# Conversion by token groups between the stages, and feed-forward products with the weights standing

## The reference, cut to what matters

```python
# first block
x = layer_norm(ALPHA * x + attention_mixer(x))      # D -> q, k, v, g ; g gates ; D -> D
x = layer_norm(ALPHA * x + retention_mixer(x))      # 8 heads of q, k (256), v, g (512)
# second block (RMS norms, modulated by c @ w_mod: scale, shift, gate of each half)
h = rms_norm(x) * (1 + scale_a) + shift_a
x = x + gate_a * (mix(h @ w_in) @ w_out)            # window and selected-key attention
h = rms_norm(x) * (1 + scale_f) + shift_f
u, g = split(h @ w_up)                              # 2 x 5632 columns
u = causal_conv3(u) + conv_b
x = x + gate_f * ((silu(u) * g) @ w_down)
out = rms_norm(x)
```

## Time and profile before

| what | value |
|---|---|
| time, median of three runs (2285.35 to 2291.1) | 2290.98 us |
| time of the profiled execution | 2291.69 us |
| span of that execution, first to last instruction | 2290.0 us |
| PE busy | 97% |
| PE weight load busy | 80% |
| DVE busy | 74% |
| ACT busy | 43% |
| mean rate of the loads | 220 GB/s |

### The profile page before, as it was taken

The page is one execution under the profiler, slowest core; times in us unless marked ns, Lnnn a source line. Parts: engine busy times, 40 slices in busy tenths (PEclk is TensorE's granted clock), DMA queues, the critical chain, the costliest instruction groups (busy, mean ns, idle before and its releaser), DMA issues.

```text
span 2290.0 us, 28816 instructions
## 1 busy us (share of the span) xinstructions
PE 2230.9 (97%) x10634; PEld 1842.1 (80%) x10634; DVE 1702.5 (74%) x1908; ACT 995.1 (43%) x1017; POOL 141.6 (6%) x202
## 2 busy tenths in 40 slices
PE   7999999999999999999999999999999999999998
PEld 6878887787888888888787778778888888888886
DVE  6788887988868878688795666985665667665567
ACT  4443433534434334343343455454444444444444
POOL 2110010010000000000011001000000000000000
PEclk9999999999999999999999999999999999999999
DMA  7877775697777777787646546455555556555653
GB/s 266 284 258 257 255 263 209 211 330 267 273 263 269 271 262 279 248 277 267 245 152 211 177 139 172 141 167 183 186 190 193 183 183 195 189 183 183 192 190 132
DMA packets 260288, 503.57 MB, mean 220 GB/s; under 512 B 14705, under 2 KB 68385, under 8 KB 259328
## 3 DMA queue, kind: packets, MB, share of 16 engines
q1 hardware_dynamic: 228480, 381.73, 50.2%
q0 software_dynamic: 31376, 119.80, 15.0%
q10 hardware_dynamic: 368, 1.18, 0.1%
HBM read 498.90 MB, written 3.69 MB: 219 GB/s over the span
## 4 chain that ended last, share of the span: by engine, by line
PE 84%; DVE 7%; DMA 3%; issue 2%; ACT 2%; SPq 0%; POOL 0%; DVEq 0%; POOLq 0%; ACTq 0%
PE pair_t L422 26%; PE pair_t L424 25%; PE pair_t L423 25%; PE turn L563 1%; DMA raw<-in_attn_w_in_dram 1%; DVE w_lo L408 1%; ACT w_hi L403 1%; PE sc L832 1%; DVE m_acc L1084 1%; PE sc L824 1%; DMA raw<-in_ret_w_in_dram 1%; PE sc L1695 1%; PE sc L682 1%; DMA raw<-in_ret_w_out_dram 0%; DVE x_mid L529 0%
## 5 line engine op out<-in xcount | busy, mean ns | idle before, releaser
L408 DVE TENSOR_TENSOR w_lo<-raw,w_hi 128x2048 fp32r<-128x2048 f32 (+1 forms) x364 | 815.6, 2243 | 461.0 <-ACT w_hi L403 456.4
L403 ACT ACTIVATE w_hi<-raw 128x2048 fp32r<-128x2048 f32 (+1 forms) x367 | 688.8, 1879 | 1029.1 <-DMA raw<-in_ret_w_in_dram 331.3
L422 PE MATMUL pair_t<-w_hi,x_hi 128*128 128x512 f32 (+1 forms) x2080 | 814.1, 391 | 18.0 <-DVE w_lo L408 12.4
L424 PE MATMUL pair_t<-w_hi,x_lo 128*128 128x512 f32 (+1 forms) x2080 | 799.6, 384 | 0.0
L423 PE MATMUL pair_t<-w_lo,x_hi 128*128 128x512 f32 (+1 forms) x2080 | 799.0, 384 | 0.0
L422 PEld LDWEIGHTS pair_t<-w_hi,x_hi 128*128 128x128 f32 x2080 | 393.6, 189 | 102.4 <-DVE w_lo L408 14.5
L424 PEld LDWEIGHTS pair_t<-w_hi,x_lo 128*128 128x128 f32 x2080 | 393.3, 189 | 78.0
L423 PEld LDWEIGHTS pair_t<-w_lo,x_hi 128*128 128x128 f32 x2080 | 393.9, 189 | 72.9 <-issue 0.2
L1084 DVE SCALAR_TENSOR_TENSOR m_acc<-m_raw,csilu,m_acc 128x1024 f32<-128x1024 f32 x180 | 230.8, 1282 | 8.0 <-DMA m_raw<-in_w_mod_dram 4.6
L422 PE MATMUL pair_t<-w_hi,f_hh 128*128 128x512 f32 x352 | 138.2, 393 | 1.5 <-DVE f_y L2278 1.0
L424 PE MATMUL pair_t<-w_hi,f_hl 128*128 128x512 f32 x352 | 137.0, 389 | 0.0
(11 more groups left out here) (364 smaller groups left out, 2143.5 us busy)
## 6 DMA issues: line engine op xcount, KB each, us to landing
m_raw<-in_w_mod_dram POOLq DMA_DIRECT2D x96, 1024.0 KB, 6.4
raw<-in_ret_w_in_dram SPq DMA_DIRECT2D x192, 512.0 KB, 4.5
raw<-in_w_up_dram SPq DMA_DIRECT2D x176, 512.0 KB, 4.2
raw<-in_w_down_dram SPq DMA_DIRECT2D x88, 512.0 KB, 4.4
raw<-in_attn_w_in_dram SPq DMA_DIRECT2D x64, 512.0 KB, 4.7
raw<-in_ret_w_out_dram SPq DMA_DIRECT2D x64, 512.0 KB, 4.8
raw<-in_w_in_dram SPq DMA_DIRECT2D x56, 512.0 KB, 4.6
raw<-in_attn_w_out_dram SPq DMA_DIRECT2D x32, 512.0 KB, 5.1
```

What stands on the lines that cost most here:

```text
L403: act.activation(chunk(w_hi, c, width), chunk(raw, c, width), ACT.Copy).then_inc(sem("hi"), 1)
L408: v.tensor_tensor(chunk(w_lo, c, width), chunk(raw, c, width), chunk(w_hi, c, width).bitcast(F32), ALU.subtract).then_inc(sem("lo"), 1)
L422: pe.matmul(to, xh, wh, start=start, stop=False)
L424: return pe.matmul(to, xl, wh, start=False, stop=stop)
```

## The change

**Layout.** x_hi and x_lo become one tensor `x_hl` in which the 256 high and the 256 low columns of a slice lie side by side.

**Borders.** The unit of conversion is now one token tile t by four slices q (4 transposes, one bank). `hi_token`, `mid_token` and `lo_token` convert it; for odd q ACT makes x_mid (four instructions of 128 columns), for even q DVE does. The first block of each stage runs by chunk and token tile in the order of `FIRST` (pairs of chunk and tile), and PE turns token tile 1 inside it, at the places shown. The orders of ACT and DVE at the borders are rewritten. The fills are 0, 44 and 0 instead of 12, 54 and 15.

**Feed-forward.** From f = 0 on for g, and from f = 1 on for u, `project_tiles` makes the product the other way: 128 x 128 of weights stand, and 512 columns (x_hi and x_lo) move against w_hi, 256 (x_hi) against w_lo. The result has features on partitions, so nothing is turned; its two halves are added (`second_halves` on ACT, `whole` on DVE). A chunk is now all of K by 128 columns and is loaded by `load_tiles` in pieces of 512 bytes. Group 0's u is still made and turned the old way.

**Attention.** In `pe_attention` the transpose of the keys moves from behind chunk 1 of the gate block to behind slice 9, and the transposes of the probabilities of heads 0 and 1 move from behind the output's second chunk to right behind the last scores, ahead of the output. Some semaphores are shared (`decay_in`, `causal_in`, `gate_in`, `fold_set`, `sel`).

```diff
--- before.py
+++ after.py
...
-        x_hi = take("x_hi", [KC, T], F32R)
-        x_lo_at = at["byte"]
-        x_lo = take("x_lo", [KC, T], F32R)
-        b_tmp = over("b_tmp", x_lo_at, [NT, CB], F32)
-        x_mid = over("x_mid", x_lo_at, [KC, T], F32)
+        x_hi_at = at["byte"]
+        x_hl = take("x_hl", [KC, 2, T], F32R)
+        x_hi, x_lo = x_hl[:, :, 0, :], x_hl[:, :, 1, :]
+        b_tmp = over("b_tmp", x_hi_at, [NT, CB], F32)
+        x_mid = over("x_mid", x_hi_at, [KC, 2, T], F32)[:, :, 1, :]
...
+        def load_tiles(sp, b, w, first):
+
+            for c in range(CH):
+                sp.wait_ge(sem("products"), CH * b + c - CH + 1)
+                for h in range(2):
+                    to = raw[:, c, 2 * h:2 * h + 2, :].rearrange("p a (b n) -> p (a b) n", n=P)
+                    src = w[:, KC // 2 * h:KC // 2 * (h + 1), bass.ds(first + c * P, P)]
                     sp.dma_start(to, src).then_inc(sem(f"chunk_in{c}"), 16)
...
+        ring = [turn[0], turn[1], sc[0], sc[1]]
+        halves_of = [turns, scs]
+
+        def project_tiles(pe, b, free, after=None):
+
+            for c in range(CH):
+                free(c)
+                pe.wait_ge(sem("lo"), CH * b + c + 1)
+                for k in range(KC):
+                    cols_of = slice(k % 4 * P, (k % 4 + 1) * P)
+                    wh, wl = w_hi[:, c, k // 4, cols_of], w_lo[:, c, k // 4, cols_of]
+                    if k:
+                        pe.matmul(ring[c][:, 0:T], wl, x_hi[:, k, :], start=False, stop=False)
+                    mm = pe.matmul(ring[c][:, :], wh, x_hl[:, k, :, :].rearrange("p a t -> p (a t)"), start=k == 0, stop=k == KC - 1)
+                    if k == 0:
+                        pe.matmul(ring[c][:, 0:T], wl, x_hi[:, k, :], start=False, stop=False)
+                mm.then_inc(sem("products"), 1)
...
+        FIRST = {1: [(0, 0), (1, 0), (0, 1), (1, 1), (2, 0), (2, 1), (3, 0), (3, 1)],
+                 2: [(0, 0), (1, 0), (2, 0), (0, 1), (1, 1), (2, 1), (3, 0), (3, 1)],
+                 3: [(0, 0), (1, 0), (0, 1), (1, 1), (2, 0), (2, 1), (3, 0), (3, 1)]}
...
+        def turn_token(pe, n, t, groups):
+
+            src = z if n == 1 else z_s
+            for q in groups:
+                token_ready(pe, n, t, q)
+                if t == 1 and q < 2:
+                    pe.wait_ge(sem("turn_hi"), group_count(n, 0, q))
+                for k in range(CH):
+                    mm = pe.transpose(group_bank(t, q)[:, k * P:(k + 1) * P],
+                                      src[:, t, (CH * q + k) * P:(CH * q + k + 1) * P], ident[:, :])
+                mm.then_inc(sem("turned"), 1)
...
+        def project_by_token(pe, b, banks, n, between):
+
+            for c, t in FIRST[n]:
+                if t == 0:
+                    pe.wait_ge(sem("lo"), CH * b + c + 1)
+                pe.wait_ge(sem("turn_lo"), group_count(n, t, c))
+                for k in range(CH):
+                    kk = CH * c + k
+                    mm = product(pe, banks[t][:, :], x_hi[:, kk, t * P:(t + 1) * P], x_lo[:, kk, t * P:(t + 1) * P],
+                                 c, k, CB, kk == 0, kk == KC - 1)
+                    if k == CH - 1 and t == 1:
+                        mm.then_inc(sem("products"), 1)
+                    between(c, t, k)
...
+        def hi_token(act, n, t, q, gain, bias):
+
+            if q % 2:
+                act.wait_ge(sem("turned"), turned_count(n, t, q))
+                for k in range(CH):
+                    kk = CH * q + k
+                    ins = act.activation(x_mid[:, kk, t * P:(t + 1) * P], group_bank(t, q)[:, k * P:(k + 1) * P],
+                                         ACT.Identity, bias=bias[:, kk:kk + 1], scale=gain[:, kk:kk + 1])
+                ins.then_inc(sem("turn_mid_a"), 1)
+            act.wait_ge(sem("turn_mid_a" if q % 2 else "turn_mid"), middle_count(n, t, q))
+            k = slice(CH * q, CH * q + CH)
+            act.activation(x_hi[:, k, t * P:(t + 1) * P], x_mid[:, k, t * P:(t + 1) * P], ACT.Copy)\
+                .then_inc(sem("turn_hi"), 1)
+
+        def mid_token(v, n, t, q, gain, bias):
+
+            v.wait_ge(sem("turned"), turned_count(n, t, q))
+            for k in range(CH):
+                kk = CH * q + k
+                ins = v.tensor_scalar(x_mid[:, kk, t * P:(t + 1) * P], group_bank(t, q)[:, k * P:(k + 1) * P],
+                                      gain[:, kk:kk + 1], bias[:, kk:kk + 1], ALU.mult, ALU.add)
+            ins.then_inc(sem("turn_mid"), 1)
+
+        def lo_token(v, n, t, q):
+
+            v.wait_ge(sem("turn_hi"), group_count(n, t, q))
+            k = slice(CH * q, CH * q + CH)
+            v.tensor_tensor(x_lo[:, k, t * P:(t + 1) * P], x_mid[:, k, t * P:(t + 1) * P],
+                            x_hi[:, k, t * P:(t + 1) * P].bitcast(F32), ALU.subtract).then_inc(sem("turn_lo"), 1)
...
-                pe.wait_ge(sem("a_krot"), i + 1)
-                if not first:
-                    pe.wait_ge(sem("a_og"), 2 * i)
-                    pe.wait_ge(sem("mod_read"), i)
-                pe_transposes(pe, sc[0], a_k, [0]).then_inc(sem("a_qk_turned"), 1)
+
+            def turn_keys(kk):
+                if kk == 9:
+                    pe.wait_ge(sem("a_krot"), i + 1)
+                    if not first:
+                        pe.wait_ge(sem("a_og"), 2 * i)
+                        pe.wait_ge(sem("mod_read"), i)
+                    pe_transposes(pe, sc[0], a_k, [0]).then_inc(sem("a_qk_turned"), 1)
...
+            def turn_second(c, t, k):
+                if (c, t, k) == (1, 0, 0):
+                    turn_token(pe, 1, 1, range(2))
+                elif (c, t, k) == (1, 0, 3):
+                    turn_token(pe, 1, 1, range(2, CH))
...
-            pe_fill(pe, turn[0], 12)
-            turn_groups(pe, 1, lambda j: normalized(pe, j), False, range(4))
+            turn_token(pe, 1, 0, range(1, CH))
             pe_retention(pe, 0)
             with pe.Fori(1, R_HEADS - 1) as i:
                 pe_retention(pe, i)
             pe_retention(pe, R_HEADS - 1)
             pe_r_output(pe, R_HEADS)
-            pe_fill(pe, turn[0], 54)
+            pe_fill(pe, turn[0], 44)
...
+            act_normalize(act, 0, range(2))
+            high(0, 0)
+            act_normalize(act, 0, range(2, CH))
             round_hi(act, R_B0, 1)
-            act_normalize(act, 1)
-            turn_hi(act, 1, False, range(0, 4))
+            high(0, 1)
+            act_normalize(act, 1, range(2))
+            high(1, 0)
+            high(1, 1)
             round_hi(act, R_B0, 2)
-            turn_hi(act, 1, False, range(4, 8))
+            for t, q in ((0, 2), (1, 2), (0, 3), (1, 3)):
+                high(t, q)
...
-                centred(0)
-                for c in range(2, CH):
-                    token_sum(1, c)
+                centred(0, range(2))
+                token_sum(1, 2)
+                scaled(0)
+                token_sum(1, 3)
                 variance(1)
-                scaled(0)
-                centred(1)
+                vec_affine(v, 2)
                 vec_rms(v, 1, 0)
+                v.wait_ge(sem("rsqrt"), 5)
+                centred(1, range(1))
+                mid_token(v, 2, 0, 0, aff[:, :], modc[:, 0:KC])
+                centred(1, range(1, 2))
+                lo_token(v, 2, 0, 0)
                 scaled(1)
...
+            def middle(t, q):
+                mid_token(v, 1, t, q, par[:, 0:KC], par[:, KC:2 * KC])
+
+            def low(t, q):
+                lo_token(v, 1, t, q)
             shift(0)
-            for c in range(2, CH):
-                token_sum(1, c)
+            token_sum(1, 2)
+            middle(0, 0)
+            token_sum(1, 3)
             variance(1)
+            low(0, 0)
             shift(1)
             zz = z[:, 1, 1024:2048]
             v.tensor_scalar(zz, zz, mv[:, 1, 0:1], rstd[:, 1:2], ALU.subtract, ALU.mult)\
                 .then_inc(sem("z_norm1"), 1)
+            split_half(v, b + 1, 1, 0)
+            split_half(v, b + 1, 1, 1)
+            low(0, 1)
+            middle(1, 0)
+            low(1, 0)
+            middle(0, 2)
+            low(1, 1)
+            split_lo(v, b + 1, 2)
+            low(0, 2)
+            middle(1, 2)
+            low(1, 2)
+            low(0, 3)
+            low(1, 3)
...
-            turn_groups(pe, 2, lambda j: scaled_copy(pe, 1, j), True, range(4))
-
-
-            project(pe, B_B0, pair[0], before=lambda c: pe.wait_ge(sem("turn_lo"), 16 + max(1, 2 * (c + 1) * (c > 0))),
-                    pairs=lambda: pe.wait_ge(sem("turn_lo"), 18),
-                    after=lambda c: pe_mod(pe, A_KV + R_HEADS - 1) if c == 3 else None,
-                    slot=turn_later(pe, 2, lambda j: scaled_copy(pe, 1, j), True))
+            turn_token(pe, 2, 0, range(CH))
+
+            def turn_second(c, t, k):
+                if (c, t, k) == (2, 0, 1):
+                    turn_token(pe, 2, 1, range(2))
+                elif (c, t, k) == (2, 0, 3):
```

(91 more changed lines are left out.)

393 lines of the change are left out of this document (188 added, 205 removed).

## The result

The change made the kernel slower: 2308.61 us as the median of four runs (2306.79 to 2312.88) beside 2291.04 us, a ratio of 1.0079 (95% interval 1.0063 to 1.0095). The forecast was 2297.1 us with a range to 2306: slower had the largest chance and came, but the medians differ by 17.6 us, nearly three times the 6.1 us of the forecast, and the time lies 2.6 us beyond the range.

A forecast was written before the change was run, and what follows sets the result against it. PE, busy 97% of the span, was taken as the bound. Feed-forward -11.3, borders +3.8 +8.2 +4.7, clock +3.2 and attention -2.5 gave +6.1 us: 2297.8 profiled, 2297.1 as median, range 2270 to 2306.

The forecast's parts named there:

- Feed-forward: Feed-forward stage: 18.6 us less for transposes, 8.5 more for matmuls, 1.2 less for a wait; net -11.3 us.
- 64 x 0.2266 + 64 x 0.1196 = 22.16 us: Feed-forward block in the new form, against 21.75 us before: 0.40 us more for each of 21 blocks, 8.5 us in all.
- rival 3: Feed-forward: chunks land too late, or 256-column matmuls beside 512 cost 0.02 us more, +27 us; 2324 us, chance 0.06.
- the cover: Feed-forward: slower 512-byte loads, copies and additions stay hidden behind PE; 0 us, ends -0 and +5.
- The chain at the borders: Three borders: conversion passing between DVE and ACT makes PE wait; +3.8, +8.2 and +4.7 us.
- The 1.8 us idle for q = 1 at border one: Border one: ACT's q = 1 conversion stands behind the rounding of chunk 1, idling PE 1.8 us.
- The wait for `x_lo` at border two: First block after retention: PE's second piece starts after 4.5 us idle, token 1's normalization being queued later on DVE.
- The clock: Gaps before chunk 3 at borders one and three: slow clock behind them adds 3.2 us in all.
- the price of 1.6 us: Clock loss behind the old 1.94 us wait at 1213.38, added for each of two gaps; ends 0 and 2.5 us.
- gaps at the start of a border and in border two end in a later wait: Borders: a later wait swallows the clock loss of these gaps, so none was added for them.
- rival 2: Borders: slower clock, first piece at border three at half pace, 2.5 us per gap, slower ACT groups; 2305 us, chance 0.14.
- Attention: Attention: transposes cover the gate copy's waits, -2.5 us (ends 0 and -2.7); the keys' wait gains 0.

The follow-up runs named there:

- the grouped form: Changed kernel with each feed-forward chunk's matmuls grouped by width (16 with w_hi, 16 with w_lo) instead of by turns: 2303.96 us, ratio 1.0055.
- early: Changed kernel with weight chunk 3 rounded and split behind group (1,2) instead of behind all groups at borders one and three: 2301.85 us, ratio 1.0053.
- hold_gap: Changed kernel with 17 fills ahead of chunk 3 at borders one and three and ahead of the m_part product at border two: 2305.09 us, ratio 1.0058.
- hold_start: Changed kernel with fills in the waits ahead of the first blocks (7 at border one, 10 at two, 4, 13 and 14 at three): 2307.91 us, ratio 1.006.
- attn_only: Kernel before the change with only the attention's new order of PE: 2291.60 us, ratio 1.0005.
- grouped_filled: Changed kernel with the old borders, feed-forward matmuls grouped by width, and fills in three old waits (9, 9 and 8): 2277.65 us, ratio 0.9927.
- no_borders_grouped: Changed kernel with the three borders as before the change and feed-forward matmuls grouped by width: 2282.46 us, ratio 0.9949.

## Why the prediction was right or wrong

**Feed-forward, wrong by 6.7 us.** The transposes are gone as counted. The step that failed is "64 x 0.2266 + 64 x 0.1196 = 22.16 us": a block takes 22.59 us. Both prices came from runs of equal matmuls, and the form sets them by turns. 6.7 ns on 1344 pairs are 9.0 us, most of the 11.3 that were forecast; rival 3 named the place but asked 20 ns. The stage missed by 6.7 us and not by 9.0, because it gained 2.3 us that the sum did not have: 0.7 of them are shorter waits for `f_y` ahead of the last outputs (1.5 us before, 0.8 after), the rest is open. Nothing of the cover failed: behind the border there is no wait for `w_lo` in the stage, for all its 512-byte loads (DMA share 0.64 from 1700 to 1770 us, 0.74 forecast), and the additions never held PE. The Trainium skill's 2.5 ns of fixed cost for a warm matmul (page "TensorE: Matmul & The Clock Gate", section "Wait — 56ns, not 53.3ns?") is not met in the grouped form either: there a matmul of 256 columns among its like takes 0.120 us, 13 ns over 0.1067.

**The chain at the borders, right in its mechanism.** The idle times ahead of chunk 3 were forecast as 4.8 and 4.6 us and are 4.49 and 4.14; `m_part` about 4, and 4.05; border two to that product +8.2, and +6.6. DVE's four x_mid instructions of 128 columns take 1.36 us (1.4 taken), ACT's 1.49 (1.5 taken). `early` shows the mechanism: with the chunk moved ahead in two queues the waits vanish at equal work. The 1.8 us idle for q = 1 at border one didn't come, because the first piece ran at half clock and took as long. The wait for `x_lo` at border two was 1.29 us, not 4.5, since ahead of the block PE had already waited 2.36 us for the scaled copy.

**The clock, wrong by 8.6 us in the profiled execution.** It cost 2.9, 1.3 and 2.5 us behind the three new waits, 1.3 and 2.1 ahead of the blocks of borders one and three, and 1.7 in the attention's output (2.1 less 0.35 for four transposes that now stand there): 11.8 us, where 3.2 were forecast. The failed step is the price of 1.6 us, from the one wait of 1.94 us, and the sentence that gaps at the start of a border and in border two end in a later wait. Behind over 4 us of waiting the slow stretch is longer: 2.9, 2.9 and 2.5 us by `hold_gap`. At border two the gap that counted is the wait for `m_part`, behind the block, where nothing swallows it; the old wait there cost something too, so only 1.3 us are new. At border three PE waited 0.93, 2.87 and 2.87 us without fills, and the first piece ran at half clock. Since token 1 is turned behind it, DVE stood idle for 6.65 us ahead of token 1's first conversion:

```profile
1559.82 1.36 DVE L592 TENSOR_SCALAR x_mid<-turn,aff,modc 128x128 f32<-128x128 f32 x4 [6.65 <-PE turn L540]
```

That is rival 2's account of the clock; `hold_start` takes 2.1 us off there. Its price of a gap (2.5 us) was nearer than the 1.6 us of the forecast. Its third term, ACT's groups at 1.9 us, did not come (1.49), and its 2305 us lack what the pairs cost. The row to read was the wait of 4.49 us at 129.59 in the kernel before, as long as the gaps forecast, with 6 us at 0.51 behind it.

**Attention, right in its stage** (-3.6 for -2.5): the waits for the gate copy are gone, and the 1.2 us for the keys became 1.2 us for `a_kT`, as was forecast. It was lost behind the stage. The wait of 2.14 us for `a_ol` was unchanged, but a slow stretch followed it (clock 0.72 from 377.5 to 383.5 us), as in all ten traces with the new order and no fills there, and not in the one trace of before (1.00 from 379.5 to 385.5 us). That a program with the same wait may or may not lose the clock behind it was not in the sum at all.

## What to carry to other kernels

Price a new idle stretch of PE by a wait of the same length in the old trace, with the slow matmuls behind it, and fill the wait if it can't be removed. Where two queues run in order and hand work to and fro, place each weight chunk by when PE wants it, between the conversions and not behind them: that alone took 11 us out of two borders here, of which 6 to 7 us arrived in the whole time. A price taken from a run of equal instructions doesn't hold for a run that alternates; if the order is free, group them.

## What the runs showed of the hardware that was not expected

- Whether the granted clock falls behind a wait of PE goes with the wait's length, and below 2.5 us the same wait is followed by it in some executions only. In the fourteen traces (behind the first 20 us), leaving out the waits for `a_pT`, which no product follows at once, a stretch at 1.2 GHz began within or just behind (2.6 us) 5 of 117 waits of 0.8 to 1.3 us, 3 of 54 of 1.3 to 1.85 us, 19 of 33 of 1.85 to 2.5 us, and 44 of 48 longer ones.
- Most of the scatter between executions of one kernel goes with the granted clock: in `attn_only` the fastest run (2288.5 us) has a mean of 0.996, the slowest (2298.2 us) 0.992, which is 0.4% of clock beside 0.4% of time. That filling three waits lessens the scatter is not shown: 5.9 us in five runs of `grouped_filled`, 5.4 in five of `no_borders_grouped`.
- A matmul of 512 columns takes 0.236 us behind one of 256, and 0.227 behind its like; one of 256 takes 0.117 on average behind one of 512, and 0.119 to 0.120 behind its like. What follows changes the 512 by less than 1 ns.
